# A two-layer decoder step in float32: the expert weights in pages with rows of 7 KB in place of 3.5 KB

## What is computed

```python
logits = (h @ w_router).astype(F32)
top_v, top_i = lax.top_k(logits, TOP_K)            # TOP_K = 2, N_EXPERTS = 8
probs = jax.nn.softmax(top_v, axis=-1)
comb = sum(one_hot(top_i) * probs)                 # (tokens, 8)
for e in range(N_EXPERTS):
    out = out + comb[..., e:e + 1] * ((silu(h @ wg[e]) * (h @ wu[e])) @ wd[e])
x = x + gt2 * out                                  # gt2: the layer's gate, per channel
```

## Time and profile before

| | |
|---|---|
| median of three runs | 1654.48 us |
| the profiled execution | 1657.53 us, span 1655.8 us |
| PE | 1603.8 us busy, 97% |
| DVE, ACT, POOL | 425.3, 157.9, 69.6 us busy |
| DMA | 535.18 MB, mean 323 GB/s |

### The profile page before, as it was taken

How to read it: one execution, slowest core, us unless ns; L and a number is a source line. 1 busy time by engine, 2 the same in 40 slices (tenths; PEclk the granted TensorE clock), 3 DMA queues, 4 the chain that set the end, 5 groups by cost and what they waited for, 6 DMA issues and landing times.

```text
span 1655.8 us, 35082 instructions
## 1 busy us (share of the span) xinstructions
PE 1603.8 (97%) x15740; PEld 1016.8 (61%) x15740; DVE 425.3 (26%) x975; ACT 157.9 (10%) x411; POOL 69.6 (4%) x118
## 2 busy tenths in 40 slices
PE   6999999999999999999999999999999999999997
PEld 3778887888887888864444445544654545444444
DVE  4478343101113883551010101010101001010114
ACT  2102301000002113030000000000000000000000
POOL 2101500000000010001000000000000000000100
PEclk8999999999999999999999999999999999999999
DMA  9998979564439877339999999999999999999994
GB/s 343 384 379 301 282 252 267 148 206 142 143 125 320 275 238 230 122 134 387 406 408 399 409 409 400 409 404 400 406 395 404 406 393 404 408 393 406 409 398 184
DMA packets 225802, 535.18 MB, mean 323 GB/s; under 512 B 17143, under 2 KB 117285, under 8 KB 212850
## 3 DMA queue, kind: packets, MB, share of 16 engines
q1 hardware_dynamic: 210162, 497.22, 80.4%
q0 software_dynamic: 8784, 29.03, 5.0%
q10 hardware_dynamic: 6704, 6.66, 1.3%
HBM read 517.47 MB, written 15.82 MB: 322 GB/s over the span
## 4 chain that ended last, share of the span: by engine, by line
PE 79%; DMA 12%; DVE 4%; SPq 3%; issue 1%; ACT 0%; DVEq 0%; POOLq 0%
PE bank L1412 29%; PE bank L1432 14%; PE bank L1073 11%; PE bank L986 9%; PE bank L1281 5%; DMA ring<-in_w_exp_up 4%; PE bank L1257 3%; DMA ring<-in_w_exp_down 2%; SPq L602 2%; PE bank L1245 2%; PE bank L994 1%; DMA ring<-in_w_in 1%; DMA area<-in_cache_k 1%; DMA ring<-in_w_exp_gate 1%; DMA area<-in_w_exp_down 1%
## 5 line engine op out<-in xcount | busy, mean ns | idle before, releaser
L1412 PE MATMUL bank<-ring,xT 128*32 128x448 f32 x3072 | 295.7, 542 | 8.7 <-issue 4.5
L1412 PE MATMUL bank<-ring,area 128*32 128x448 f32 x3072 | 293.6, 539 | 3.2 <-issue 2.4
L483 DVE TENSOR_TENSOR area<-bank,area 128x224 f32<-128x224 f32 x96 | 54.2, 564 | 783.3 <-ACT area L939 783.1
L1073 PE MATMUL bank<-hT,ring 128*128 128x264 f32 x1024 | 240.0, 390 | 3.2 <-DMA ring<-in_w_in 2.4
L1412 PEld LDWEIGHTS bank<-ring,xT 128*32 128x32 f32 x3072 | 112.9, 110 | 183.8 <-issue 180.5
L1412 PEld LDWEIGHTS bank<-ring,area 128*32 128x32 f32 x3072 | 122.5, 110 | 166.1 <-issue 151.6
L1432 PE MATMUL bank<-area 128*32 128x256 f32 x3840 | 216.0, 379 | 3.0 <-issue 2.5
L1073 PEld LDWEIGHTS bank<-hT,ring 128*128 128x128 f32 x1024 | 193.8, 192 | 38.9 <-issue 3.7
L1432 PEld LDWEIGHTS bank<-area 128*32 128x32 f32 x3840 | 139.6, 110 | 72.7 <-DMA area<-in_w_exp_down 2.7
L986 PE MATMUL bank<-hT,ring 128*128 128x264 f32 x704 | 157.4, 386 | 0.0
L986 PEld LDWEIGHTS bank<-hT,ring 128*128 128x128 f32 x704 | 133.7, 190 | 23.2 <-issue 0.4
(11 more groups left out here) (304 smaller groups left out, 883.8 us busy)
## 6 DMA issues: line engine op xcount, KB each, us to landing
ring<-in_w_exp_gate SPq DMA_DIRECT2D x256, 448.0 KB, 16.4
ring<-in_w_exp_up SPq DMA_DIRECT2D x256, 448.0 KB, 15.3
area<-in_w_exp_down SPq DMA_DIRECT2D x64, 1024.0 KB, 18.1
ring<-in_w_ada SPq DMA_DIRECT2D x96, 512.0 KB, 9.7
ring<-in_w_in SPq DMA_DIRECT2D x32, 1024.0 KB, 13.0
ring<-in_w_exp_down SPq DMA_DIRECT2D x32, 1024.0 KB, 15.7
area<-in_w_exp_down SPq DMA_DIRECT2D x32, 512.0 KB, 18.5
ring<-in_w_ff_gate SPq DMA_DIRECT2D x22, 512.0 KB, 6.8
```

The source lines that it names most:

```text
L483: dve.tensor_tensor(F["act_tok"][:, t, :].rearrange("p (i n) -> p n i", i=BODY), bank[t][:, SLICE:2 * SLICE].rearrange("p (n i) -> p n i", ...
L1073: mm = pe.matmul(bank[b][:, 0:T], w[:, c, :], hT[:, c, :], start=(c == 0), stop=(c == DC - 1))
L1412: mm = pe.matmul(bank[t][32 * g:32 * g + 32, 0:2 * SLICE].rearrange("p (s n) -> p s n", s=2), tokens[:, t, 32 * r:32 * r + 32], w[:, :, SL ...
```

## The change

Turns are twice as wide and half as many: `BODY` is 14 (rows of down per turn), `WIDE` 1,792 columns, `TURNS` 16. `SPAN` = 7 keeps the old width for the ring of down rows (7 slots) and for the branch `Else`.

- A gate or up page is now 128 x 1,792 floats, a row of 7,168 B in two neighbouring slots; sixteen slots hold eight of them, thus four steps.
- Gate and up have banks of their own (0 to 2 and 3 to 5), one product of 448 columns each; down adds up in banks 6 and 7.
- The down products of turn m-1 stand between the steps of turn m, one to two rows after each step. SP's order alternates in the same way.
- Routing and gates are all spread in turn 0. `silu_tok` and `act_tok` lie in other tiles' places, `act_tok` in that of `h_tok`; so ACT and DVE wait for the scatter of `h_tok` first.
- For the prompt rows of expert 7 the gate is multiplied into y before the scatter.
- At the start the state transposes move behind z 3 and z 5, POOL's constants and state behind z 0, and ACT brings one block of constants more.

```diff
-BODY = 7
+BODY = 14
+SPAN = 7
+SPANS = FE // P // SPAN
-ERING = 2 * DC + BODY
+ERING = 2 * DC + SPAN
+        STATE_AT = (3, 5)
+        DOWN_PAGES = ((0, 2), (2, 2), (4, 2), (6, 1), (7, 2), (9, 2), (11, 2), (13, 1))
+        DOWN_ROWS = ((0, 1), (2, 3), (4, 5), (6,), (7, 8), (9, 10), (11,), (12, 13))
...
+            def gate_up_pages(m, r):
+                e, b = m // BODIES, m % BODIES
+                for half, w in ((0, A["w_exp_gate"]), (1, A["w_exp_up"])):
+                    k = (2 * r + half) % DC
+                    if m == 0 and r < DC // 2:
+                        sp.wait_ge(s.pages_used, STRAIGHT - RING + 2 * k + 2)
+                    else:
+                        sp.wait_ge(s.gu_used, DC * m + r - DC // 2 + 1)
+                    sp.dma_start(run(eslot[2 * k], 2)[:, 0:WIDE],
+                                 w[0, e, r * P:(r + 1) * P, b * WIDE:(b + 1) * WIDE]).then_inc(page_in[eslot[2 * k]], 16)
+            def down_rows_in(m, i, n):
...
+                at = eslot[2 * DC + i % SPAN]
+                if m or i >= SPAN:
+                    sp.wait_ge(s.d_used, BODY * m + i - SPAN + n)
...
+                sp.dma_start(run(at, n), rows[:, i * D:(i + n) * D]).then_inc(page_in[at], 16)
+            for r in range(DC // 2):
+                gate_up_pages(0, r)
+            sp.wait_ge(s.routed, 1)
+            most = sp.value_load(most_i[0:1, 0:1], min_val=0, max_val=T)
+            with sp.If(most < CAP + 1):
+                for m in range(TURNS + 1):
+                    for r in range(DC):
+                        if m < TURNS and (m or r >= DC // 2):
+                            gate_up_pages(m, r)
+                        if m:
+                            i, n = DOWN_PAGES[r]
+                            down_rows_in(m - 1, i, n)
...
+            def gate_up_step(m, r):                 # PE
+                for half in range(2):
+                    k = (2 * r + half) % DC
+                    at = eslot[2 * k]
+                    pe.wait_ge(page_in[at], landed[at] + 16 * (2 * m + (2 * r + half) // DC + 1))
+                    w.append(run(at, 2)[:, 0:WIDE])
+                for t in range(TILES):
+                    if r == 0 and m:
+                        pe.wait_ge(s.act_e, TILES * (m - 1) + t + 1)
...
+                    for half in range(2):
+                        for g in range(4):
+                            mm = pe.matmul(bank[t + 3 * half][32 * g:32 * g + 32, 0:SLICE], tokens[:, t, 32 * r:32 * r + 32],
+                                           w[half][:, SLICE * g:SLICE * (g + 1)],
+                                           start=(r == 0), stop=(r == DC - 1), skip_group_check=True)
...
                 for m in range(TURNS + 1):
-                    if m < TURNS:
-                        gate_up_turn(m)
...
+                    for r in range(DC):
+                        if m < TURNS:
+                            gate_up_step(m, r)
+                        if m == 0:
+                            if r == 1:
+                                pe.wait_ge(s.wt_ready, 1)
+                                turn_routing()
+                            if r == 2:
+                                spread_routing(E - 1)
+                            if r == 4:
+                                spread_gate(False)
+                            if r == 5:
+                                spread_gate_by_strips()
+                            if r == 6:
+                                spread_gate(True)
+                        else:
+                            for i in DOWN_ROWS[r]:
+                                down_row(m - 1, i)
...
+                dve.wait_ge(s.d_used, BODY * TURNS)
+                dve.tensor_tensor(y_gated[:, 0:2, :], bank[6][:, :].rearrange("p (t n) -> p t n", t=2),
+                                  gate.broadcast_to([P, 2, S]), ALU.mult).then_inc(s.y_gated, 1)
...
-                    base(dve.tensor_tensor(y_out[:, 0:2, n], bank[(0, 1, 2, 5)[q]][:, :].rearrange("p (i n) -> p i n", i=2),
-                                           gate_tok[:, n].unsqueeze(1).broadcast_to([P, 2, S]), ALU.mult))
-                    dve.tensor_tensor(y_out[:, 0:2, n], y_out[:, 0:2, n], x_tok[:, :, n], ALU.add).then_inc(s.final_out, 1)
+                    dve.tensor_tensor(y_out[:, 0:2, n], bank[(0, 1, 2, 5)[q]][:, :].rearrange("p (i n) -> p i n", i=2),
+                                      x_tok[:, :, n], ALU.add).then_inc(s.final_out, 1)
...
-            pool.wait_ge(s.pages_used, 12)
-            pool.dma_start(cst[:, 2 * P:lo], const_in[:, 2 * P:lo]).then_inc(s.rest_in, 16)
+            pool.wait_ge(s.pages_used, used_up("z", 0, 0))
+            pool.dma_start(cst[:, 3 * P:lo], const_in[:, 3 * P:lo]).then_inc(s.rest_in, 16)
...
-                    if l == 0 and i < LAYERS:
-                        if i == 0:
+                    if l == 0 and i in STATE_AT:
```

More of the change, by code:

```diff
@@ L227, in build @@
         x_tok = flat["fT"][:, 0:2 * D].rearrange("p (i d) -> p i d", i=2)
-        x_tok_s = flat["silu"][0:NS, 0:D]
+        for name, v in (("silu_tok", flat["silu"]), ("act_tok", flat["h_tok"])):
+            FFN[name] = v[:, 0:TILES * SLICE].rearrange("p (t n) -> p t n", t=TILES)
+        x_tok_s = bias[0:NS, :, :].rearrange("p h n -> p (h n)")
         gate_tok = flat["act"][:, 0:D]
         gate_tok_s = flat["h_tok"][0:NS, 2 * D:3 * D]
-        picked = [[v[:, i * D:(i + 1) * D] for i in range(2)] + [flat["h_tok"][0:NS, j * D:(j + 1) * D]]
+        picked = [[v[:, i * D:(i + 1) * D] for i in range(2)] + [(cst[0:NS, P:P + D], FFN["pick_s"])[j]]
                   for j, v in enumerate((hT_flat, sq_flat))]
@@ new lines, in _ @@
+            with sp.Else():
+                for k in range(DC):
+                    sp.wait_ge(page_in[eslot[2 * k]], landed[eslot[2 * k]] + 16)
+                with sp.Fori(0, E) as e:
+                    for b in range(SPANS):
+                        n = e * SPANS + b
+                        for r in range(DC):
+                            for half, w in ((0, A["w_exp_gate"]), (1, A["w_exp_up"])):
+                                at = eslot[2 * r + half]
+                                sp.wait_ge(s.gu_used, n * DC + (r + 1))
+                                sp.dma_start(wide(at)[:, 0:SPAN * P],
+                                             w[0][bass.ds(e, 1), r * P:(r + 1) * P, b * SPAN * P:(b + 1) * SPAN * P].rearrange(
+                                                 "o p n -> (o p) n")).then_inc(page_in[at], 16)
+                        for i in range(SPAN):
+                            at = eslot[2 * DC + i]
+                            sp.wait_ge(s.d_used, n * SPAN + (i + 1))
+                            sp.dma_start(wide(at), A["w_exp_down"][0][bass.ds(e, 1), b * SPAN * P:(b + 1) * SPAN * P, :].rearrange(
+                                "o (p i) d -> (o p) i d", i=SPAN)[:, i, :]).then_inc(page_in[at], 16)
@@ L1399, in gate_up_turn @@
                 e = m // BODIES
                 tokens = h_got[e % 2]
[L1401 to L1410 removed]
+                w = []
@@ new lines, in gate_up_step @@
+                for half in range(2):
+                    k = (2 * r + half) % DC
[5 more added lines that the diff above has]
+                        pe.wait_ge(s.act_e, TILES * (m - 1) + t + 1)
+                    if r == 0 and m % BODIES == 0:
+                        pe.wait_ge(s.h_got_out, TILES * e + t + 1)
+                    for half in range(2):
@@ new lines, in gate_up_step, with down_row @@
+                mm.then_inc(s.gu_used, 1)
+            def down_row(m, i):
+                e, b = m // BODIES, m % BODIES
+                if i == 0:
+                    pe.wait_ge(s.turned, TILES * (m + 1))
+                    if m == 0:
+                        pe.wait_ge(s.gate_tok_out, 5)
+                    if b == 0 and e:
+                        pe.wait_ge(s.y_out, 2 * e)
+                at = eslot[2 * DC + i % SPAN]
+                if i in [first for first, _ in DOWN_PAGES]:
+                    pe.wait_ge(page_in[at], landed[at] + 16 * (2 * m + i // SPAN + 1))
+                for t in range(TILES):
+                    for q in range(4):
+                        mm = pe.matmul(bank[6 + t // 2][32 * q:32 * q + 32, (t % 2) * S:(t % 2 + 1) * S],
+                                       FFN["actT"][:, m % 2, t, 32 * i:32 * i + 32], wide(at)[:, q * S:(q + 1) * S],
+                                       start=(b == 0 and i == 0 and t != 1), stop=(b == BODIES - 1 and i == BODY - 1),
+                                       skip_group_check=True)
+                mm.then_inc(s.d_used, 1)
```

254 lines of the change are left out of this document (109 added, 145 removed).

## The result

The kernel after takes 1642.2 us, the median of 4 runs (1640.29 to 1645.29), beside 1655.07 for the kernel before in the same rounds: ratio 0.9927, 95% interval 0.9912 to 0.9942. The forecast was 1642. The profiled execution had 1645.29 us on a span of 1643.6, against 1655.8 before.

What follows compares the result with a forecast made beforehand. DMA rate was taken to bound the experts from 750 to 1617 us, PE the end. Rows -16.8, coarse pages +3 and +4.5, end -3.1, start -0.5 summed to -12.9 us from 1654.48: 1642, range 1628 to 1656.

Steps and rivals of the forecast that it cites:

- What bounds: In the experts, DMA rate bounds 750 to 1617 us, and PE's rest of 20.4 us bounds the end.
- Rows of 7 KB, -16.8: Gate and up transfers in the experts: longer rows raise 403.7 GB/s to 416.1, -16.8 us, bounds 0 and -24.
- the 8.4 ns: Fixed cost of each transfer row on an engine, beside 0.0373 ns a byte, taken from pairs of windows.
- Rival 1: In the experts, longer rows bring no rate and the coarse pages' cost remains: 1658 us, slower; 15%.
- Rival 2: In expert transfers, packet overhead is half as large, 3.7 ns a row: gain 7.4 us, 1651 us; 17%.
- Coarse pages at the start, +3: Start of the experts: slots free later while engines are half idle, 3 us of DMA time lost, bounds 0 to 5.
- Coarse pages at the end, +4.5: End of the experts: longer PE and DVE work after the last gate page; with the start's cost, bounds 2 to 7.
- PE's order costs nothing: In the experts, alternating gate and up products with down products adds no PE time; 27.10 us per old turn.
- The forecast's floor for PE: Experts on PE alone would end at 1616.7 us: 741.8 + 867.2 + 6.7 + 1.0.
- End, -3.1: Kernel's end: gate multiplied into y before the scatter leaves less DVE work behind it, -3.1 us, bounds -2 and -3.5.
- Start, -0.5: Kernel's start: no wait for w_in page, -2.4, but later router, +1.9: -0.5 us, bounds -2.4 and +3.
- Rivals 3 and 4: 3: PE becomes the bound, 1627 us, 9%. 4: moved state and turn 0's waits stall PE several us, 1648 us, 9%.

Runs made afterwards that it cites:

- thin kernels: About half of PE's products in the experts left out: kernel before 1643.92 us, kernel after 1635.69, kernel after with gate and up pages in two transfers 1651.47.
- b_split: Kernel after with each gate or up page in two transfers of 3,584 B rows: 1661.3 us, ratio 1.0029 to before.
- l_padded: Kernel after with 64 idle semaphore increments on SP behind its last transfer: 1637.17 us, ratio 0.9889 to before.
- h_small: Kernel after with all products, but expert transfers cut to 512 B a partition from the third turn on: 1631.02 us.
- i_oldstart: Kernel after with the old start (POOL's small loads before z 0, state transposes behind z 0 and z 1): 1640.06 us, ratio 0.9917 to before.
- a_again: Kernel after once more, unchanged: 1641.66 us, ratio 0.9928 to before.
- d_oldend: Kernel after with the old end, y scattered unscaled and multiplied by the gate behind the scatter: 1643.64 us, ratio 0.9935 to before.
- j_down3: Kernel after with down pages in six transfers a turn, two with 12 KB rows, in place of eight: 1641.49 us, ratio 0.9937 to before.

## Why the prediction was right

- *What bounds*: right. Cutting the transfers takes the kernel before to 1629.7; cutting PE's work leaves it at 1643.9. Both resources are close.
- *Rows of 7 KB, -16.8*: right. Split rows give back 19.6 us between medians and 16 to 18 in the experts of the profiles; the thin kernels give 14 to 19. That all of it is a cost per row (the 8.4 ns) isn't shown: part of it may be a cost per transfer, since no run changes one without the other. Rival 1 (rows bring no rate, 1658) has its price about confirmed by b_split, 1661.3, and its premise refuted. Rival 2, a gain of 7.4 us, falls too. The Trainium skill ("DMA: Bandwidth & Descriptors", "Why small descriptors are slow") has about 3 cycles of overhead a packet beside one cycle per 32 bytes, by which the estimate for these rows was 1.3%. The thin kernels disagree: 2.2% is seen over all bytes, which is more on the gate and up bytes alone.
- *Coarse pages at the start, +3*: the hole was there (390 and 385 GB/s in the two windows from 750 to 782, against 415 and 412 before: 0.84 MB, 2 us), but for another reason in large part. The page of step 4 was issued 6.06 us into the experts, not 4.7, because PE's stream was slow there. In l_padded it is issued after 4.78 us (744.02), as forecast, and 399 and 421 GB/s flow: 0.16 MB less in the first ten, more than before behind them. So the 3 us were mis-sized: the pages themselves cost nearly nothing, and about 2 us came from the slow stretch, which the forecast didn't have.
- *Coarse pages at the end, +4.5*: from the last step's begin to the last product 26.7 us against 4.5 + 20.7 + 1.0 = 26.2; the wait on the transposes is 0.55 in place of 1.0. DVE's product of 448 columns takes 0.96 us (1.13 was the upper bound):

```profile
L496 DVE TENSOR_TENSOR area<-bank,area 128x448 f32<-128x448 f32 x48 | 45.9, 956 | 577.5 <-ACT area L981 577.5
```

- *PE's order costs nothing*: right for the alternation (54.21 a turn). The forecast's floor for PE left out the slow stretches, 2.6 and nearly 4 us in h_small, which no row of before showed.
- *End, -3.1*: right, 15.0 to 12.0.
- *Start, -0.5*: the mechanisms came as told (no more wait for w_in, a wait of 2.20 us for the router where 1.9 was forecast), but the size isn't settled. All ten profiles with the new start have the same work up to the experts, and these begin at 736.0 to 744.0, 738.9 in the mean, behind a wait for the router of nothing to 2.3 us; in the four with the old start they begin at 739.3 to 741.8, 740.3 in the mean. That is 1.4 us for the new start, inside the forecast's bounds and far inside the spread. Between i_oldstart and l_padded, two kernels without slow stretches, lie 2.9 us of median in its favour, with intervals that touch, on two chips.
- *Rivals 3 and 4*: neither decides. PE does pace turns 1 to 6, though at a full DMA share, and between its floor (880.8) and the measured 889.5 only 9 us are left to the transfers. Rival 4's stall exists at 2.2 us, inside the forecast.

The sum agreed to 0.2 us, and a part of that is luck: two errors offset each other. The forecast had no slow stretches, and it took the rest of the change in the experts for less than it is. In the profiles the experts last 889.5, 887.8 and 889.9 us with the stretches (after, a_again, d_oldend) and 886.0 and 886.6 without (i_oldstart, l_padded), so they cost 1 to 4 us there; less than the 8 us of h_small, since the transfers set the pace later on. And l_padded's span is 17.9 below that of before: start 2.6, experts 12.4 (886.6 us), end 2.9. Its experts gain 12.4 where the forecast had 9.3; the 3 us for the pages at the start are what it charged too much. By medians l_padded is 4.5 us below a_again. The profiles explain only part of that: the profiled run of l_padded is its slowest and that of a_again its fastest, and the former is 1.8 us the longer, by its later start.

What stays open: the spread of runs of one kernel (1637.9 to 1646.1 in a_again, 1639.0 to 1647.8 in j_down3, which has no slow stretches), why the granted clock at the start differs, what opens and closes the gaps in PE's instructions, and how the cost of a short row splits between row and transfer.

## What to carry to other kernels

Where transfers are the bound, the length of their contiguous rows is a term of its own even above 3.5 KB (here together with the size of the transfers, 896 KB in place of 448), and pairs of windows in the old trace price it. Whether few slots suffice depends on how their use is spread in time: work out, for each slot, the time from its release to the next use against the landing time. And when a version comes out a few tenths of a per cent off, look for "issue" gaps on PE before blaming the edit: in the one comparison made here, 64 idle instructions in another engine's program went with a median 4.5 us lower, more than the 3 us of the new end.

## What the runs showed of the hardware that was not expected

- PE's stream of instructions ran with gaps (11.58 us for 9.02 of work, 5.72 for 2.59) at the end of six indirect transfers of POOL. With 64 instructions added to SP's program the gaps were gone; the median was 0.3 to 0.4% lower, the experts of the profiles 1.2 to 2.9 us shorter.
- The granted clock between 30 and 35 us was 0.52 in one run and 0.95 in another of the same kernel, and the start of the experts moved by up to 5.8 us; only 2.8 of these are in by z 0.
- A wait of 3.3 us was followed by a granted clock of 0.51 over 6 us, and 48 products took 5.35 us in place of 2.80, nearly as much again as the wait. Of 16 waits in the same place nine were followed by slower products, and the longest, 3.7 us, was not.
- One core moved 414 GB/s for 513 us with most rows of 7 and 8 KB, against 405 with the gate and up rows halved and their transfers doubled in number.
